# Four conditioning rows of an RWKV step placed in two pairs

## The reference, cut to what matters

```python
def _ada(c, w, b):
    mod = jax.nn.silu(c) @ w + b          # (2048) @ (2048 x 6144)
    shift, scale, gate = jnp.split(mod[:, None, :], 3, axis=-1)

def step(S, inp):                          # RWKV-7, per head, both directions
    r_t, w_t, k_t, v_t, kk_t, a_t = inp
    sa = -jnp.einsum('dbhvk,dbhk->dbhv', S, kk_t)
    S = (S * w_t[..., None, :] + sa[..., :, None] * (kk_t * a_t)[..., None, :]
         + v_t[..., :, None] * k_t[..., None, :])
    return S, jnp.einsum('dbhvk,dbhk->dbhv', S, r_t)
```

## Time and profile before

| | us |
|---|---|
| median of 3 runs | 2788.41 |
| lowest and highest | 2785.87, 2789.18 |
| the profiled execution | 2788.39 |
| its span (first to last instruction) | 2786.3 |
| the RWKV steps 0 to 7 in it | about 384 to 660 |
| TensorE busy | 2625.2 (94% of the span) |
| VectorE busy | 1942.2 (70%) |
| ScalarE busy | 1185.9 (43%) |

### The profile page before, as it was taken

The page is one execution under the profiler, slowest core; times in us unless marked ns, Lnnn a source line. Parts: engine busy times, 40 slices in busy tenths (PEclk is TensorE's granted clock), DMA queues, the critical chain, the costliest instruction groups (busy, mean ns, idle before and its releaser), DMA issues. The chain is left out here.

```text
span 2786.3 us, 40763 instructions
## 1 busy us (share of the span) xinstructions
PE 2625.2 (94%) x17014; PEld 2151.8 (77%) x17014; DVE 1942.2 (70%) x1885; ACT 1185.9 (43%) x1375; POOL 272.1 (10%) x199
## 2 busy tenths in 40 slices
PE   3999979998999999999999899999999999999996
PEld 3888857776777888888888678888778888888885
DVE  5788856666566888888888878865668755555557
ACT  2555544445444333333333345555443333333332
POOL 0000000000004000000000085641040000000000
PEclk9999989999999999999999999999999999999998
DMA  8899743230647888888888366744468755555552
GB/s 308 313 331 344 287 136 129 97 120 16 241 164 262 327 304 328 303 323 307 317 312 308 121 227 242 271 155 160 166 231 323 253 193 191 186 195 186 190 193 79
DMA packets 259411, 636.60 MB, mean 228 GB/s; under 512 B 10607, under 2 KB 17445, under 8 KB 239173
## 3 DMA queue, kind: packets, MB, share of 16 engines
q1 hardware_dynamic: 253106, 621.84, 62.7%
q10 hardware_dynamic: 6162, 12.72, 1.2%
HBM read 632.42 MB, written 2.10 MB: 228 GB/s over the span
## 5 line engine op out<-in xcount | busy, mean ns | idle before, releaser
L521 DVE TENSOR_TENSOR s_wl<-s_raw,s_wh 128x2048 fp32r<-128x2048 f32 (+1 forms) x393 | 914.5, 2327 | 513.6 <-ACT s_wh L516 504.8
L516 ACT ACTIVATE s_wh<-s_raw 128x2048 fp32r<-128x2048 f32 x396 | 758.5, 1916 | 1080.8 <-PE pa L726 412.7
L724 PE MATMUL pa<-s_wh,s_hth 128*128 128x512 f32 x1312 | 526.2, 401 | 14.8 <-DVE s_wl L521 7.9
L725 PE MATMUL pa<-s_wl,s_hth 128*128 128x512 f32 x1312 | 515.1, 393 | 0.0
L726 PE MATMUL pa<-s_wh,s_htl 128*128 128x512 f32 x1312 | 514.8, 392 | 0.0
L724 PEld LDWEIGHTS pa<-s_wh,s_hth 128*128 128x128 f32 x1312 | 248.9, 190 | 76.7 <-DVE s_wl L521 13.1
L726 PEld LDWEIGHTS pa<-s_wh,s_htl 128*128 128x128 f32 x1312 | 248.7, 190 | 53.7
L725 PEld LDWEIGHTS pa<-s_wl,s_hth 128*128 128x128 f32 x1312 | 249.4, 190 | 48.7
L724 PE MATMUL pb<-s_wh,s_hth 128*128 128x512 f32 x704 | 274.1, 389 | 0.0
L726 PE MATMUL pb<-s_wh,s_htl 128*128 128x512 f32 x704 | 273.9, 389 | 0.0
L725 PE MATMUL pb<-s_wl,s_hth 128*128 128x512 f32 x704 | 273.9, 389 | 0.0
(11 more groups left out here) (398 smaller groups left out, 3482.4 us busy)
## 6 DMA issues: line engine op xcount, KB each, us to landing
s_raw<-in_ffn_w_in SPq DMA_DIRECT2D x176, 1024.0 KB, 5.2
s_adaw<-in_ada_w SPq DMA_DIRECT2D x144, 1024.0 KB, 6.0
s_raw<-in_ffn_w_out SPq DMA_DIRECT2D x88, 1024.0 KB, 7.7
s_raw<-in_ab_w_in SPq DMA_DIRECT2D x48, 1024.0 KB, 9.8
s_raw<-in_diff_w_in SPq DMA_DIRECT2D x48, 1024.0 KB, 5.2
s_adaw<-in_ada_w SPq DMA_DIRECT2D x48, 512.0 KB, 6.1
s_raw<-in_ab_w_out SPq DMA_DIRECT2D x16, 1024.0 KB, 5.3
s_qkv<-in_ada_w SPq DMA_DIRECT2D x16, 1024.0 KB, 7.2
```

Source lines behind the costliest of these rows:

```text
L516: act.activation(wh[:, s % 2, :, 0:width], raw[:, s, :, 0:width], ACT.Copy).then_inc(hi_done, 1)
L521: dve.tensor_tensor(wl[:, s % 2, :, 0:width], raw[:, s, :, 0:width], wh[:, s % 2, :, 0:width].bitcast(F32), ALU.subtract).then_inc(lo_done, 1)
L724: pe.matmul(o, a_hi, w_hi, start=start and k == 0, stop=False)
L725: pe.matmul(o, a_hi, w_lo, start=False, stop=False)
```

## The change

For a step with four rows the first two are issued at place 1, one right behind the other, and the last two at place 3. In step 3 the two rows, which stood at places 2 and 3, both stand at place 3; in step 7 the two rows, which stood at places 0 and 1, both stand at place 1. `rows_turn` stays at place 0 of step 3 and place 3 of step 7. No row is added or left out, and no other function is touched. Each row is issued at its old place or at the one after it.

```diff
             def rows_at(t, at):
 
                 b = sum(ROWS_IN[i] for i in range(-2, t))
-                if t == 3:
-                    if at == 0:
-                        rows_turn(pe, 0)
-                    mine = (at - 2,) if at >= 2 else ()
-                elif t == PAIRS - 1:
-                    if at == 3:
-                        rows_turn(pe, 1)
-                    mine = (at,) if at < ROWS_IN[t] else ()
-                else:
-                    mine = (at,)
-                for i in mine:
-                    row_products(pe, b + i)
+                if (t, at) in ((3, 0), (PAIRS - 1, 3)):
+                    rows_turn(pe, 0 if t == 3 else 1)
+                elif at == 1 or at == 3:
+                    for i in range(2 if ROWS_IN[t] == 2 or at == 1 else 4)[-2:]:
+                        if ROWS_IN[t] == 4 or at == (3 if t == 3 else 1):
+                            row_products(pe, b + i)
```

## The result

| | before | changed |
|---|---|---|
| median of 18 runs, us | 2788.07 | 2794.66 |
| lowest and highest | 2783.57, 2793.87 | 2791.36, 2796.29 |
| profiled execution, span | 2786.3 | 2794.2 |

The ratio is 1.0021, with a 95% interval of 1.0014 to 1.0029: the changed kernel is slower by 3.9 to 8.1 us, 0.21% in the middle. The forecast was 2793.6 us, +5.2 us.

The account below looks back on a forecast made before the run. The RWKV steps were taken as bound by TensorE's row of instructions, loosely tied to VectorE and ScalarE. Steps 1, 2, 5, 6 2.2, step 0 1.72, step 3 0.82, step 4 0.3, step 7 0.14: +5.2 us, 2793.6; range 2790.0 to 2797.0.

Parts of the forecast that it names:

- The cover at place 2: Place 2's row covers VectorE's chain to line 2001, all but 0.04 us; moving it to place 3 nets +0.82 us a step.
- its sign: New TensorE waits for line 2001 before the scores, steps 1 to 6: 0.8 to 1.1 us each, 0.5 in step 4.
- Place 0 to place 1: Steps 1, 2, 4, 5, 6: 1.13 us removed at place 0, 0.86 added at place 1, net -0.27 us.
- Step 0: Places 0 and 2 give back 0, since waits were open there; places 1 and 3 cost 0.86 each: +1.72 us.
- Step 4: Hitch inside its place-2 row: +0.02 us if it falls in the wait, +0.55 if on the path; +0.3 taken.
- Step 6: A regular step with four rows: -0.27 us at places 0 and 1, +0.82 at places 2 and 3, +0.55 together.
- Step 7: Mixed with gated attention: place 0 gives 0, a 0.72 us wait at place 1 takes in all but 0.14 us.
- The transfers: Both loads of a pair start together on SyncE's queue, land in 4.7 to 6.2 us, with 17 us available: cost 0.
- rival C: The granted clock falls where TensorE idles in the steps, 1.5 us lost per fall: 2795.1 to 2798 us; chance 0.07.
- B: VectorE's chain gives way, place 2 is no cover; 14 pairs save 0.27 us each: 2784.6 us, -0.14%; chance 0.07.
- D: A pair's second load comes late, TensorE stands at place 3 or 1; 1 us at three pairs gives 2796.6; chance 0.03.
- the line of 0.2%: Smallest change a measurement of this kernel can tell from no change: 5.6 us, that is 2794.0 us.

Follow-up runs that it names:

- again: The changed kernel run once more beside the kernel before on the same chip: 1.0022 (1.0013 to 1.0031), +6.1 us, profiled span 2788.2 us.
- loads apart: Changed kernel with the second load of each pair held back until a later level's V is copied: 1.0020 against the kernel before, +5.6 us.
- only place 3: Kernel before with only the last two rows of a step paired at place 3 (step 3 too), places 0 and 1 as before: 1.0019, +5.3 us.
- the pairs elsewhere: Pairs at places 0 and 2 (step 3: both at 2, step 7: both at 0), none at 1 and 3: 1.0007 against the kernel before.
- with the pair split: Changed kernel with the pair at place 1 split by the turning of the keys: 1.0019 against the kernel before (1.0022 for the changed kernel).
- the pairs stand closer: Pairs at places 1 and 2, 7 us apart, none at 0 and 3: 1.0021 against the kernel before, +5.9 us.

## Why the prediction was right, step by step

The length of a step, from `first` (the first matmul behind place 3) to the next `first`, by the order of time of each kernel's profile, in us:

| step | before | changed | again | loads apart | only place 3 | forecast | again - before |
|---|---|---|---|---|---|---|---|
| 0 | 27.76 | 29.75 | 29.49 | 29.68 | 28.80 | +1.72 | +1.73 |
| 1 | 35.84 | 36.56 | 36.56 | 36.56 | 36.71 | +0.55 | +0.72 |
| 2 | 36.45 | 39.00 | 37.09 | 37.03 | 37.31 | +0.55 | +0.64 |
| 3 | 34.91 | 35.77 | 35.77 | 35.77 | 35.77 | +0.82 | +0.86 |
| 4 | 36.97 | 37.03 | 37.10 | 37.36 | 37.32 | +0.3 | +0.13 |
| 5 | 36.45 | 37.03 | 37.03 | 37.04 | 37.31 | +0.55 | +0.58 |
| 6 | 35.18 | 35.52 | 35.52 | 35.51 | 35.80 | +0.55 | +0.34 |
| sum | 243.56 | 250.66 | 248.56 | 248.95 | 249.02 | +5.0 | +5.0 |

- **The cover at place 2** was the step on which all rested, and it held: taken away, the row gave TensorE almost nothing (step 3, which has no other move, lost 0.86 us, its second row whole), and a wait for line 2001 appeared: 0.83 to 0.87 us in steps 1, 3, 5 and 6, 0.58 in step 0. In steps 2 and 4 the standstill ahead of it had used the time up. So the waits come to 4.0 us in the change, not the 6 or so that the prediction named as its sign; with the loads apart, where steps 2 and 4 have theirs, they come to 5.7.
- **Place 0 to place 1** gave back 0.27 us where forecast, by steps 2, 5 and 6: with only place 3 changed steps 2 and 5 take 37.31 and step 6 35.80; with both halves they take 37.03 to 37.09 and 35.52 (the first profile's step 2 apart, where the clock fell). In step 1 it gave 0.15, not 0.27 (36.71 against 36.56). In step 1 the row of before is followed by the head sums themselves (128x256), not by the 64x64 turning of the previous output, so that it stood between two other shapes; the price of the earlier trace rows was for another neighbour. That this is the reason was not tried.
- **Step 0** came out at 1.73, with the wait for the squares grown by 1.0 to 1.3 us in place of the row's 1.1, as forecast.
- **Step 4**, taken as 0.3 between 0.02 and 0.55, gave 0.06, 0.13 and 0.39. Both orders have a hitch there, 0.5 us in the earlier trace rows and 1.0 in the repeated profile, where the new wait took it in for the most part. With the loads apart step 4 has no standstill by name, but is still 0.32 us longer than step 5: a product at 532.06 us takes 0.62 us where its neighbours take 0.28. What that smaller hitch is, no run shows.
- **Step 6** lost 0.34, not 0.55. The kernel before has a small hitch there: one product at 622.00 us takes 0.47 us where its neighbours take 0.28, so that the step is about 0.2 us longer than it would be without. Against 35.18 - 0.2 the loss is 0.54. What the hitch is, no run shows.
- **Step 7** and what is behind: the pair at place 1 was taken in but for about 0.1 us as forecast. From `first` at its start to the turning of the sum it took 35.74 us before and 35.81 in the repeat.
- **The transfers**, forecast at 0, were the one step argued from too little. No row waits for its load in the changed kernel, and to that extent it was right. But their landing went from 4.7/4.9/6.2 us (least, median, most) to 4.9/6.1/8.3, and what they hold up is not the rows but TensorE's instructions. In the changed kernel this cost next to nothing (step 2 took 37.09 us with the standstill and 37.03 without), since the standstills fell ahead of the wait that was there anyway. That no price was paid is luck: the prediction had not seen the standstills, nor that its own wait would hide them. With the pairs elsewhere they came to 3.4 us.
- **The size.** Steps 0 to 6 give 5.0 us in the repeat, as in the forecast. That the sum fits better than its terms is in part luck: steps 1 and 2 came out 0.17 and 0.09 us above their terms, steps 4 and 6 0.17 and 0.21 below. The ratios of the runs gave 5.9, 6.1 and 5.6 us (the last with the loads apart; 6.6, 4.7 and 5.9 by the medians), and each of these intervals holds 5.2. Whether the 1 us that is left is anything can't be told. The first profile shows what could be in it: step 2 took 39.00 us in place of 37.09, and step 7 with its fallen stretch 38.08 in place of 35.81, together 4.2 us more, most of it by the clock. The fall in step 7 is not the change's. Ten of the thirteen profiles have one in that step, 3.4 us or more long, among them the kernel before with only lines 1999 and 2001 exchanged, which has the old order and single loads (the 5 us ahead of the fall and the fall, in the form of the stretches above):

```profile
625.70:630.70 5.00, 4.76 (x60) 3.68 (x60) 3.02 (x8) 3.76 (x6) 0.00 (x0) 0.96 0.23 93
630.70:634.10 3.40, 3.40 (x68) 3.33 (x70) 1.65 (x4) 0.04 (x1) 0.00 (x0) 0.56 0.03 7
```

There TensorE had been busy for 4.76 of the 5 us before the fall. The fall at 475.5 followed a standstill of 1.16 us at once, and the only other one in step 2 (with the pair split) followed one of 2.10 us, while three profiles with standstills of 0.88 to 0.92 us there had none; whether the one brings the other was not tried. By the prediction's own sign, a granted clock below 1.00 in the steps, the first profile spoke for rival C. The repeat, without a fall and as slow by the runs, shows that C is a cost of some executions and not the cause.
- **Rivals B and D** are out: B by the wait itself and by the half-change at place 3, D by its absence in the change's waits. D's price shows only where the pairs stand closer, or where the loads alone were paired (1.3 us in step 0).

The forecast put the most likely time just under the line of 0.2%, and the measured median lies 0.7 us past 2794.0; the interval holds both.

## What to carry to other kernels

A piece of filling work in front of a wait costs nothing there as far as it covers the wait, and its whole length at a place where nobody is waited for: before it is moved, look at what the next instructions need and by how much they now miss the wait; a start that follows its releaser's end by only 0.1 us (473.38 to 473.47 us in the earlier trace rows) can be a wait that is hidden, not one that is absent. Grouping such pieces saves the change of shape (0.27 us of 1.13 here), so if they are grouped, then at the place where they are cover; that this gains time on the whole was not shown here. And when the users of transfers are grouped, look at what the transfers do: here two at once held up instructions, and spreading them again took nearly all of the standstills away.

## What had not been expected of the hardware

TensorE's own instructions come over the same transfer engines as the data. Each packet of queue 8 has 16 KB. The trace does not name the engine that one is for, but the counts point to TensorE: in the steps of the kernel before there is one packet for each 251 of TensorE's recorded matmuls and weight loads, while VectorE, ScalarE and GpSimd together have 636 instructions there.

In the profile of the changed kernel two loads of 1 MB filled 90% of the transfer engines for 5.9 us, the packet behind them came after 435 of TensorE's instructions in place of at most 352 in the kernel before, and TensorE stood still for 1.16 us. In the traces of all runs, each of the 19 standstills inside a group of equal matmuls, 0.2 to 2.1 us long, ended 1.2 to 1.6 us behind the end of a packet of this queue. All but two of them (0.4 and 0.2 us) stood where two row loads were under way together (1.5 us in the kernel before by that alone), and spreading the loads took both of the changed kernel's away. Not every pair of loads brings one: the kernel with the pair at place 1 only has none by name.

The Trainium skill, "Runtime: NRT & Kernel Launch", Instruction fetch mechanics, says that instructions are fetched in blocks of 16 KiB over a DMA queue while the current ones run, and that the cost is mostly hidden. The block size agrees with the packets of 16 KB. Hidden it was in the kernel before, by name at least, but not always with two loads at once.
